# Mixing product, query norm and first query tile by halves of the tokens, and the first head picked alone ahead of the expert rows

## The reference

```python
mixed = g[:, :, 0, :] * y_att + g[:, :, 1, :] * y_conv
x = x + mixed @ w_out[i]                               # mixing product
h2 = rms_norm(x, ffn_norm_g[i])                        # query norm
x = x + peer(h2, w_peer_q[i], peer_sub_keys[i], peer_u[i], peer_v[i])
...
def peer(h, w_query, sub_keys, expert_u, expert_v):
    q = (h @ w_query).reshape(B, S, PEER_HEADS, 2, PEER_HALF)      # 8 heads
    sc = jnp.einsum('bshcd,hckd->bshck', q, sub_keys)              # scores
    sv, si = lax.top_k(sc, PEER_TOPK)                              # 16 of 128, twice a head
    ...
    top_s, top_j = lax.top_k(cand_s, PEER_TOPK)                    # pick: 16 experts a head
    eidx = jnp.take_along_axis(cand_i, top_j, axis=-1)
    gate = jax.nn.softmax(top_s, axis=-1)
    u = expert_u[et]; v = expert_v[et]                             # rows
    act = jax.nn.gelu(jnp.einsum('tnd,td->tn', u, xt)) * gt        # dots
    return jnp.einsum('tn,tnd->td', act, v)                        # sums
```

## Time and profile before

| | us |
|---|---|
| median of three runs | 1561.72 (1559.27, 1561.72, 1562.13) |
| span of the profiled execution, first to last instruction | 1554.9 |
| PE busy | 1212.9 (78%) |
| DVE busy | 926.5 (60%) |
| ACT busy | 431.5 (28%) |
| POOL busy | 347.1 (22%) |
| mean granted TensorE clock (share of full speed) | 0.878 |
| DMA, mean over the span | 264 GB/s |

### The profile page before, as it was taken

One profiled execution on the slowest core, in us unless ns is written; L12 is line 12 of the kernel. 1 busy time (PEld: TensorE's weight loads), 2 busy tenths in 40 slices (PEclk: granted clock), 3 DMA queues, 4 the chain that ended last, 5 costly groups with the idle time before them and its releaser, 6 DMA issues.

```text
span 1554.9 us, 26679 instructions
## 1 busy us (share of the span) xinstructions
PE 1212.9 (78%) x11282; PEld 834.9 (54%) x11282; DVE 926.5 (60%) x2067; ACT 431.5 (28%) x1094; POOL 347.1 (22%) x315
## 2 busy tenths in 40 slices
PE   7989898894385533457856775799987888999998
PEld 6467784772153100125524452468877774888843
DVE  2887666657797988785677655321455343455512
ACT  2111420132432422543364332423243211110100
POOL 1000012034354555454455544000000000000000
PEclk9997999996597855569878996899999999999999
DMA  9551459699999999999999999624300023344432
GB/s 381 195 191 66 144 205 390 238 383 419 414 410 420 420 422 421 421 414 419 416 421 420 420 418 418 240 82 163 109 9 3 4 111 108 122 163 161 137 140 104
DMA packets 109720, 409.73 MB, mean 264 GB/s; under 512 B 8456, under 2 KB 33552, under 8 KB 76448
## 3 DMA queue, kind: packets, MB, share of 16 engines
q0 software_dynamic: 44576, 297.35, 46.5%
q1 hardware_dynamic: 63552, 106.48, 19.2%
q10 hardware_dynamic: 1472, 4.20, 1.0%
HBM read 405.89 MB, written 2.11 MB: 262 GB/s over the span
## 4 chain that ended last, share of the span: by engine, by line
PE 58%; DMA 22%; DVE 10%; ACT 4%; issue 3%; POOL 2%; another core or an unknown queue 0%; POOLq 0%; DVEq 0%; ACTq 0%; SPq 0%
PE psum L502 20%; DMA arena<-in_experts,arena 17%; PE psum L1942 8%; PE psum L2454 5%; PE psum L512 4%; DVE arena L1490 4%; PE psum L1521 3%; DMA arena<-in_lora_up 2%; PE psum L755 2%; PE psum L1269 2%; POOL arena L1475 2%; PE psum L2244 2%; PE psum L760 2%; DMA arena<-in_ada_wT 2%; PE psum L741 2%
## 5 line engine op out<-in xcount | busy, mean ns | idle before, releaser
L1475 POOL DMA_INDIRECT arena<-in_experts,arena x256 | 317.1, 1239 | 383.2 <-PE psum L1521 299.8
L1521 PE MATMUL psum<-arena 128*32 128x512 f32 x1024 | 185.4, 805 | 238.2 <-ACT arena L1506 231.6
L502 PE MATMUL psum<-actT,weights 128*128 128x256 f32 x1312 | 287.3, 381 | 0.0
L502 PEld LDWEIGHTS psum<-actT,weights 128*128 128x128 f32 x1312 | 250.3, 191 | 35.7 <-issue 1.5
L1521 PEld LDWEIGHTS psum<-arena 128*32 128x32 f32 x1024 | 22.7, 121 | 329.5 <-ACT arena L1506 307.3
L1490 DVE CUSTOM_DVE_ANT_0 arena<-arena 128x1024 f32<-128x1024 f32 x96 | 116.7, 1224 | 50.9 <-DMA arena<-in_experts,arena 50.1
L1490 DVE CUSTOM_DVE_ANT_0 arena<-weights,arena 128x1024 f32<-128x1024 f32 x96 | 116.6, 1223 | 37.1 <-DMA arena<-in_experts,arena 35.1
L1496 ACT ACTIVATE arena<-arena 128x2 f32<-128x2 f32 x128 | 26.1, 204 | 364.3 <-DVE arena L1490 350.4
L1942 PE MATMUL psum<-arena 64*64 64x64 f32 (+1 forms) x2816 | 89.7, 231 | 17.4 <-DVE arena L2059 7.1
L1942 PEld LDWEIGHTS psum<-arena 64*64 64x64 f32 x2816 | 84.1, 142 | 26.0 <-issue 14.6
L1490 DVE CUSTOM_DVE_ANT_0 arena<-normed,arena 128x1024 f32<-128x1024 f32 x64 | 77.2, 1225 | 22.1 <-DMA arena<-in_experts,arena 20.3
(11 more groups left out here) (390 smaller groups left out, 1897.0 us busy)
## 6 DMA issues: line engine op xcount, KB each, us to landing
weights<-in_w_in SPq DMA_DIRECT2D x18, 2048.0 KB
arena<-in_ada_wT POOLq DMA_DIRECT2D x48, 512.0 KB, 6.3
weights<-in_ffn_w_up SPq DMA_DIRECT2D x22, 1024.0 KB
weights<-in_ffn_w_down SPq DMA_DIRECT2D x5, 2048.0 KB
weights<-in_w_out SPq DMA_DIRECT2D x4, 2048.0 KB
weights<-in_w_peer_q SPq DMA_DIRECT2D x4, 2048.0 KB
arena<-in_experts,arena POOLq DMA_INDIRECT x256
weights<-in_w_ple_gate SPq DMA_DIRECT2D x2, 2048.0 KB
```

Of the source, the lines that this page charges most:

```text
L502: mm = nc.tensor.matmul(out[:, c * T:(c + 1) * T], w[:, k, c * P:(c + 1) * P], act[:, k, :], start=(k == 0), stop=(k == kc - 1))
L1475: nc.gpsimd.indirect_dma_start(out=rows[:, n % RING, :], out_offset=None, in_=dram["experts"], in_offset=bass.IndirectOffsetOnAxis(ap=eidx ...
L1521: mm = nc.tensor.matmul(SUMS[sum_part(k, i), i, :], diag[:, pos, :], rows[:, pos, D + 512 * i:D + 512 * (i + 1)], start=first, stop=last, ...
```

## The change

- Mixing product: TensorE waits for both w_out tiles and both accumulators, multiplies block 0 of both tiles, then block 1 in pieces between the later steps.
- The tile `peer_q0` goes to a third slot in the arena (behind the mixed tokens), requested right behind `mix_out1`.
- The query norm goes block by block (`act_query_half`, `act_query_root`, `dve_query_diag`, `pe_query_turn`, `act_query_turn`), and so does the product with `peer_q0`, by 128 columns; scores of heads 0 and 1 of block 0 follow head by head (`first_scores`).
- `dve_first_heads` picks head 0 alone and hands out its 16 expert numbers, then adds block 1's last half, takes the first piece of head 1, block 1's diagonal and normed rows, and then the rest of head 1.
- POOL may request the first rows on head 0's numbers; row 5, whose slot lies on the third weight slot, waits for the whole first query product; row 16 waits for head 1.
- The normed tokens are staged in the query buffer; POOL (block 0) and SP (block 1) write them out, and POOL instead of ScalarE loads them back in the form that the dots want.
- Modulation steps move forward, by other counts of `some(n)`. Some semaphores are merged.

Core of the diff:

```diff
 def pe_mix(pe):
     ...
-            pe.wait_ge(S("mix_ok"), 4)
-            for i in range(2):
-                pe_tokens(pe, f"mix_out{i}", mixT)
+            pe.wait_ge(S("mix_ok"), 2)
+            tile = [pe_tile(pe, f"mix_out{i}") for i in range(2)]
...
+            mixed(0, 0, 0, DC // 2)
+            pe.wait_ge(S("mix_ok"), 4)
+            mixed(0, 0, DC // 2, DC).then_inc(S("first_pe"), 1)
+            mixed(1, 0, 0, DC).then_inc(S("first_pe"), 1)
+            mixed(0, 1, 0, DC // 2)
+            pe_query_turn(pe, 0, range(0, 4))
+            mixed(0, 1, DC // 2, DC).then_inc(S("tile_done"), 1)
+            pe_query_turn(pe, 0, range(4, DC))
+            mixed(1, 1, 0, 2)
+
+            w, out = pe_tile(pe, "peer_q0")
...
+            pe.wait_ge(S("query_turned"), DC)
+            query(0, 0)
+            query(1, 0).then_inc(S("first_pe"), 1)
+            mixed(1, 1, 2, 3)
+            pe.wait_ge(S("keys_in"), 16)
+            first_scores(0)
+            query(2, 0)
+            query(3, 0).then_inc(S("first_pe"), 1)
+            mixed(1, 1, 3, 4)
+            first_scores(1)
+            mixed(1, 1, 4, DC).then_inc(S("tile_done"), 1)
+            pe_spread_first(pe, "e", 0)
+            pe_query_turn(pe, 1, range(0, 2))
...
+            pe.wait_ge(S("query_turned"), TB * DC)
+            for c in range(4):
+                mm = query(c, 1)
+            mm.then_inc(S("tile_done"), 1)

 def sp_weights(sp):
...
+                if name == "peer_q2":
+                    sp.wait_ge(S("norm_dve"), norm_at("dve", "n2", "row1"))
+                    sp.dma_start(normed_rows[P:T], staged[:, 1, :]).then_inc(S("last_tokens"), 16)
...
-                if i >= WSLOTS:
+                if name == "peer_q0":
+                    sp.wait_ge(S("lg_sub"), TB)
+                elif i >= WSLOTS:
                     sp.wait_ge(S("tile_done"), i - WSLOTS + 1)

 def dve_first(dve, st):
...
-            some(8)
+            some(12)
...
                 if b:
                     dve.wait_ge(S("pt_pe"), b)
-                    some(2)
+                    some(5)
...
+                if b:
+                    some(2)
                 dve.wait_ge(S("lg_pe"), b + 1)
...
-            some(7)
+            some(9)
...
-            some(10)
-            add_product(dve, "mix_out", "x1", lambda: some(8))
+            some(3)
+            for i in range(2):
+                dve.wait_ge(S("first_pe"), i + 1)
+                dst = halves_of(xres, 0, i)
+                nc.vector.tensor_tensor(dst, toks(G[tile_at[f"mix_out{i}"] % 2])[:, 0, :], dst, ALU.add).then_inc(
+                    S("norm_dve"), 1)
+                if i == 0:
+                    some(5)

 def dve_queries(dve, st, mod):
...
+            add_last_mixed(dve, 0)
+        def dve_first_heads(dve, st):
...
+            dve.wait_ge(S("first_act"), 2)
+            all_of(dve_pick(st, sc[0], 0, 0, 1))
+            indices(0)
+            add_last_mixed(dve, 1)
+            dve.wait_ge(S("first_act"), 4)
+            second = dve_pick(st, sc[0], 1, 1, 1)
+            next(second)
+            dve_query_diag(dve, 1)
+            dve_query_row(dve, 1)
+            all_of(second)
+            dve_gate_shift(st, 0, HEADS)
+            indices(1)
+            dve_gates(dve, st, 0, HEADS)

 def pool_rows(pool):
...
+                if n == 0:
+                    pool.wait_ge(S("eidx_ok"), 1)
+                elif n == PK:
+                    pool.wait_ge(S("eidx_ok"), 2)
...
+                if n == THIRD_ROW:
+                    pool.wait_ge(S("tile_done"), tile_at["peer_q0"] + 1)
```

More of the change, by code:

```diff
@@ L282, in build @@
         mixT = chunks(DC)
+        third = Region(r.at).take(4096)
         toep = r.take(AH * T).rearrange("p (s t) -> p s t", s=AH)
@@ L886, in pe_mix, with mixed @@
                 pe_features(pe, f"att_out{i}", attT)
-            pe.wait_ge(S("mix_ok"), 4)
-            for i in range(2):
-                pe_tokens(pe, f"mix_out{i}", mixT)
+            pe.wait_ge(S("mix_ok"), 2)
+            tile = [pe_tile(pe, f"mix_out{i}") for i in range(2)]
+            def mixed(i, b, first, last):
+                w, out = tile[i]
+                for k in range(first, last):
+                    mm = nc.tensor.matmul(out[:, b * 512:(b + 1) * 512], mixT[:, k, b * P:(b + 1) * P], w[:, k, :],
+                                          start=(k == 0), stop=(k == DC - 1))
+                return mm
@@ L1152, in build, with picked, scored @@
         assert TURNS * RING == NSEL and RING % QUADS == 0 and GROUP * 2 == QUADS
+        FIRST_SCORES = [AUX[:, 2 + h, 0:2 * NK] for h in range(HEADS)]
+        THIRD_ROW = 5
+        def picked(turn):
+            return turn + 2
+        def scored(i, b):
+            return TB * i + b
         def rows_ahead(b, t, g):
@@ new lines, in pe_queries, with pe_scores @@
+            next(chunk)
+            pe_scores(pe, 0, 1)
+            pe_spread_first(pe, "e", 1)
+            next(chunk)
+            for h in range(HEADS):
+                pe_spread_first(pe, "g", h)
+            all_of(chunk)
+            for b in range(TB):
+                pe_scores(pe, 1, b)
+            all_of(pe_features_by_chunk(pe, f"peer_q{QUARTERS - 2}", actT))
+        def pe_scores(pe, i, b):
+            wait_freed(pe, f"peer_q{i}")
+            if i > 1 or i and b:
+                pe.wait_ge(S("sc_cp"), scored(i - 1, b))
+            for g in range(4 * i, 4 * i + 4):
+                mm = nc.tensor.matmul(AUX[:, score_bank(i, b), (g % 4) * P:(g % 4 + 1) * P],
+                                      qpT[:, g, b * P:(b + 1) * P], keysT[:, g, :], start=True, stop=True)
+            mm.then_inc(S("sc_pe"), 1)
@@ L1305, in act_queries @@
+            act_query_root(act, 1)
+            act_query_turn(act, 1, range(DC))
+            nc.scalar.copy(qpT[:, 0:4, P:T], feat(product(act, "peer_q0"))[:, :, P:T]).then_inc(freed("peer_q0"), 1)
+            act.wait_ge(S("ada_used"), 6 * DC)
+            act_scores(act, 0, 1)
             for _ in act_select(act, 0, 0):
@@ new lines, in dve_select @@
+        def dve_select(dve, st, b, quarter):
+            turn = QUARTERS * b + quarter
+            dve.wait_ge(S("sc_cp"), scored(quarter, b))
+            for _ in dve_pick(st, sc[b], HEADS * quarter, 0, HEADS):
+                yield
+            dve_gate_shift(st, 0, HEADS)
+            for h in range(HEADS):
+                if h:
+                    yield
+                dve_experts(st, h)
+            dve_spread_e(dve, slice(0, HEADS * PK))
+            yield
+            dve_gates(dve, st, turn, HEADS)
```

426 lines of the change are left out of this document (242 added, 184 removed).

## The result

The changed kernel takes 1576.38 us (median of four, 1576.2 to 1577.29) against 1560.84 for the kernel before in the same runs: a ratio of 1.0105 (95% interval 1.0090 to 1.0119), 15.5 us slower. Forecast was slower by 5.5 us.

A forecast was written before the change was run, and what follows sets the result against it. The prediction took DMA bytes for expert rows as the bound: 32 us later turn minus 28 preloaded gives +4, taken as +5.5; span 1554.9 becomes 1560.4, and 6.8 from span to median gives 1567 us, range 1553 to 1577.

The forecast's parts named there:

- What bounds the kernel: Row stretch, about 315 to 975 us: DMA saturated, only bytes count; 669 us, of which 640 are rows.
- (a): Modulation steps ahead of the second block's logits: logits 4.4 us later, at 193.5; last attention product ends at 243.5.
- (b): Mixing product waits for both w_out tiles: starts 10.5 us after the attention product, at 254 instead of 242.3.
- (c): Mixing product in halves, head 0 picked early: first row asked for at about 298, 20 us earlier.
- (d): Block 1's norm and the query products after head 0's pick: first sums at 349.2, 15 us later.
- Rival 3: TensorE at half clock through the small pieces: ring turns at 360 to 363, 1577 to 1580 us; chance 0.15.
- ring: Eight slots for expert rows, freed by TensorE's sums; forecast to start turning at 350.3 instead of 318.26.
- context gate: VectorE's wait for the context during the rows: a later one counted as nothing, bounds 0 to +5 us.
- (e): DMA sum over the rows: ring turns 32 us later, 28 loaded beforehand, +4, taken as +5.5.
- The prediction's own sign of being wrong: Row stretch behind the ring's start: the prediction is wrong if it is not 641 us long.
- rival 1: TensorE reaches the rows early enough: ring turns before 344.8 for a gain, about 1557 or 1552 us; chance 0.25.

The follow-up runs named there:

- e3: The changed kernel with modulation steps at the second block's logits put back to two, the others moved behind logits and mixed tokens: ratio 1.0109.
- e10: e7 with modulation steps at the second block's logits put back to two, the other five behind the mixed tokens: ratio 0.9973.
- e1: The changed kernel with the first query tile's request held back until the second w_out tile has landed: ratio 1.0148.
- e4: The changed kernel with the lora weights asked for ahead of the first context tile instead of behind the second: ratio 1.0092.
- e5: The kernel before with the lora weights asked for ahead of the first context tile: ratio 0.9999.
- e6: The changed kernel with the edits of both e2 and e4: ratio 1.0020.
- e2: The changed kernel with TensorE starting both blocks on the first w_out tile alone, then waiting for the second: ratio 1.0073.
- e7: e6 with the third query tile's product in pieces between the first groups of rows, and the context load earlier: ratios 0.9958 and 0.9983.

## Why the prediction was right and wrong

**What bounds the kernel**: right. In the changed kernel the DMA misses 19 us more than before in the windows from 315 to 465, and the rows end 22 us later; the versions that close the holes end sooner.

**(a), logits**: +4.4 forecast, +4.9 measured (the fifth step waited 1.52, taken as 1). But the slower TensorE behind the wait was taken as 0.5 and cost 3.0: transposes 3.68 instead of 1.97, at a granted clock of 0.50 (1.2 GHz), the products behind them 4.66 instead of 3.33. e3 and e10 show besides that putting the steps back, to the two places tried, did not win this term back.

**(b), the second tile**: a term that was mis-sized. 10.5 us after the attention product was taken; the wait was 14.36. With (a) that makes the mixing product 7 us later than forecast (260.91 against 254). e1 rules out the query tile as the cause. The rest of the first tile, which landed 10.4 us after its own request, at 249.5, and the six modulation loads asked for between 243 and 253 fit: at 420 GB/s the tile and six loads take 12.5 us together, an estimate from the earlier trace rows. e3, with nine such loads asked for between 241 and 260, points the same way (15.85), but this was not tried by itself.

**(c) and (d), from the mixing product to the sums**: right in length. Forecast 95.2 us from its start to the first sums (254 to 349.2), measured 94.25. (Block 0's turns are 8 products, not 16; with 16 query products and seven mixing products among them they took 12.2 us to the first scores, as forecast.) The first row came 5 us later than forecast, by the same delay.

Rival 3 came true in a small part. TensorE had little to do from 300.8 until block 1's turns at 305.61; then the granted clock was 0.50 until 313, and 1.00 from 316 on. Block 1's turns took 2.08 and 2.05 us where block 0's took 1.05 each, and its 32 query products 9.55 where block 0's took 7.55: 4 us, most of which the forecast's terms allowed for. The second query product and the third ran at the full clock. Rival 3's time, 1577 to 1580, is nearly what was measured, but by luck: its ring turned at 360 to 363, not at 356, and the context gate had no part in it.

**(e), the sum on the DMA**: the step that failed is "A later context gate is taken up by eight rows that lie ready; I count nothing". The gate cost about 6.6 us. It is the other way round: with rows that lie ready, VectorE reaches the gate earlier after the first sums (58.7 us after, from 355.16 to 413.86, against 62.8 before, from 334.42 to 397.25), while the context comes as long after them as before (68.0 against 67.3). It waits longer, and this time with a ring that has landed in full (POOL's wait of 14.84 us), so that the DMA dries up. e4, e5 and e6 show it: asking for the lora weights early gives 9.3 us on the rows' end in the changed kernel, 6.8 on top of e2, and nothing in the kernel before. The ring also turned more slowly at first than the sum had it, with row 10 at 364.58, since TensorE does scores and a piece of a query product between the first groups; the first two groups lay as far apart before (334.42 and 342.49), but then the DMA still had rows to load. The prediction's own sign of being wrong came true here: the stretch behind the ring's start, to be 641 us long, took 653 (356.2 to 1009.3).

Without these two the sum comes out close: e6 has no gate, its ring turns at 349.45, where the forecast had 350.3, and its rows end 6.2 us later than before, where the forecast had 5.5; the ratio is 1.0020 (1.0007 to 1.0034) against the forecast's 1.0035. Some of that is luck, since the DMA misses 10 us in the windows from 315 to 375, not the 16 of the sum. For an earlier turn the sum doesn't hold: with the ring turning at 333 to 335 it gives a gain of 10 to 11 us, and e7 gained 5.4 and 3.7.

**The rivals**: rival 1's point, the ring's turn at 344.8, was the right thing to look at, and e7 crosses it (333.46 to 335.14) by another way, moving a product rather than speeding one up. On the path to the first sums the granted clock fell at three of TensorE's waits: to 0.50 after 4.88 us ahead of the transposes, after 14.36 us ahead of the mixing product (260.9 to 263), and ahead of block 1's turns. The traces agree there with the rule that the prediction cites from the Trainium skill ("TensorE: Matmul & The Clock Gate", "Loop structure matters more than you think"); but the slow stretches cost 3, about 1 and 4 us, not the whole chain at half speed.

## What to carry to other kernels

Where a stretch is bound by transfers through a ring of few slots, an earlier first request gains only if the consumer also comes earlier, or the ring merely fills and stands; find the consumer's first use and move work from ahead of it to between its first turns. A wait that is free beside a full DMA is not free once buffers lie ready: look for the next fixed arrival behind the place that was sped up. And when a product needs two tiles, start on the one that is there, in an order in which its work covers the other's landing.

## What the runs showed beyond expectation

The second w_out tile, 2 MB, kept TensorE waiting for 14.36 us after its request could be made, with or without 2 MB more asked for behind it in the same queue (14.82 in e1), which fits a queue that serves its tiles in order: the query tile landed 5.3 us after it, about what 2 MB take at 420 GB/s. The half megabyte of lora weights took 34.03 us behind a weight tile beside the rows; asked for ahead of the first context tile in e4, it was no longer waited for. Moving modulation steps by a few places changed nothing in the end, twice over (e3, e10): a 1 MB weight tile beside their loads took over 11 us to land instead of 5 to 7, and what VectorE had won was given back.
